# Two hybrid transformer blocks on one core: a spare PSUM bank for a grouped projection's third member, two heads' decays issued after the first linear-attention cores, ScalarE rounding some weights, and one side block moved up

## Chip, cores and metric

One core of one Trainium2 chip runs the whole program. The metric is the device time of one execution in microseconds (us), the median of the runs shown.

## The reference, cut to what matters

The input is one sequence of 512 tokens with 1024 features, float32. Two stacks of two layers follow each other.

- The first stack, per layer: RMS norm with modulation, one wide projection, an RWKV-7 recurrence over 8 heads of 64 (written with chunks of 128 tokens in the kernel), a multi-scale pooling branch, two gated projections, an output projection, and a gated feed-forward network (hidden size 2816).
- The second stack, per layer: RMS norm, one wide projection, gated linear attention (GLA) with 4 heads (key 128, value 256) in both directions, grouped-query attention with 8 query heads, two sigmoid gates, an output projection, a feed-forward network, and a gated side input.

What matters for the change, in the reference's terms (the second stack's GLA branch):

```python
la_f = (jax.nn.log_sigmoid(ra_f @ w_alpha_up[0] + b_alpha[0]) / GLA_TAU).reshape(b, s, GLA_HEADS, GLA_DK)
cum = jnp.cumsum(la, axis=3)
q_dec = q * jnp.exp(cum)
k_intra = k * jnp.exp(-cum)
scores = jnp.where(mask, jnp.einsum('nbhid,nbhjd->nbhij', q_dec, k_intra), 0.0)
o_gla = rms_norm_2(o_f + o_b, g_gla_out)
branch_a = (o_gla * jax.nn.silu(gg)) @ w_o_gla
mixed = jax.nn.sigmoid(gate_a) * branch_a + jax.nn.sigmoid(gate_b) * branch_b
```

The decays of a head (`la`, `cum`) are needed before that head's scores, and the norm of a head's output before its gated output.

## The kernel before, in words

**Weights.** Every large matrix is streamed in 128x128 blocks, four blocks to a chunk, through a ring of 8 slots. SyncE issues a chunk's DMA when the chunk 8 places earlier has been used up (L2265). GpSimd then makes two fp32r tensors of it: `w_hi`, the rounded weight (L2241), and `w_lo`, the rest (L2243), which is written over `raw`. The activations are split in the same way into `_hi` and `_lo`. A block costs three matmuls of 128x512: hi by hi, lo by hi, hi by lo (`linear`, L420 to L422). A projection is 8 blocks, 24 matmuls.

**PSUM.** There are 8 banks. `BANKS` names pools over them: `lin` (banks 0, 1, 2), `bg` (3), `aux` (4 to 7), and in the second stack `lin2` (0, 1) and `bg2` (2, 3). `begin(name, pool)` takes a pool's next bank in turn, and makes TensorE wait until the bank's last reader is done: semaphore `bankN_read` is raised by the instruction that reads the bank last.

**Order.** There is no scheduler: each engine's program is written out by hand, and engines meet at semaphores only. TensorE goes through projections, small matmuls of the recurrences and "side jobs". A side job is a projection whose result is stored to DRAM by ScalarE for later use (`gates_before`, L1114), and whose blocks `fill(n)` deals out, n at a time, at places where TensorE would wait: 8 blocks to a job, L485 to L487.

**Groups.** `group` (through `stepped`, L444, L445, L452) runs the first three projections behind a norm together, block by block, as the norm's output tiles arrive. It is called twice in each layer: for projections `M_WA, M_GL, M_GLV` and the first three of the feed-forward network (`fg0, fu0, fg1`) in the first stack, for `ra, gq, gk` and the first three `pg` of the side input in the second.

**The recurrence of the first stack** (`wkv_chunk`, 4 chunks of 128 tokens in each layer): small matmuls alternate with copies on ScalarE (`gm`, L1236) and products on VectorE (`mt`, L1861, L1863), with one to six fill blocks between them.

**GLA.** TensorE first issues for heads 0 and 1 the projections (`gla_in`: gq, gk, gv, and gg 0 and 1), among them the decay matmuls of all four heads (`gla_decay`, L834, two jobs `gz` each, pool `aux`). ScalarE turns each into logs (L1362 to L1369), VectorE scans them. Then come the cores (`gla_core`), heads 0 to 3, with `gla_in` of head h + 2 behind core h. A core is ten `aux` jobs: two transposes (L846), two scores (L853), three states (L863, L865), `fill(6)`, two outputs `go` 0 and 1 (L877 to L881), `fill(2)`, and the sums of squares `gn` (L888, L889). Then ScalarE takes the root (L1047), VectorE the reciprocal (L1605), and only the product at L2035 releases the bank of `go` 0. In front of each core stand `FILL_CORE[h]` fill blocks. ScalarE makes the factors of head 0 (`gla_factors`, L1380 to L1384) after it has read the last gg projection of `gla_in` 1. Behind core 3 the rest of the first eight side jobs (g2a) is filled, and the output projection `p2a` reads the split head outputs `go_hi`, `go_lo` (L1592).

Of the kernel before, what the change touches and what calls it, by code (L numbers as in the profile page):

```python
# [21 lines left out]
ALU = mybir.AluOpType  # L22
ACT = mybir.ActivationFunctionType
# [36 lines left out]
FILL_SCORE = (0, 2, 0, 5)  # L60
FILL_MEAN = (16, 13)
FILL_POOL = 8
FILL_CORE = (5, 2, 2, 15)
# [57 lines left out]
def emit(nc, known, wstream, ada_slabs, xT, c_rows, cols, consts, rope, inv_count, small, out):  # L121
# [5 lines left out]
    with ExitStack() as ctx:  # L127
# [160 lines left out]
        windows_at = []  # L288

# [68 lines left out]
        def _(pe):  # L358
# [22 lines left out]
            def close(name):  # L381
                closed[name] = len(closed)
                for s in touched:
                    chunk_end[s] = done(name)
                touched.clear()
# [80 lines left out]
            def group(members, key):  # L466

                stepped(members, key, ("lin",) * len(members), "lin")
# [3 lines left out]
            def side_jobs(members, pool):  # L472

                side["jobs"], side["at"], side["pool"] = members, 0, pool
# [212 lines left out]
            def block1(l):  # L687
# [55 lines left out]
                fill(FILL_PREP[l])  # L743
                for c in range(NCH):
                    wkv_chunk(l, c)
# [168 lines left out]
            def block2(l):  # L914
# [4 lines left out]
                side_jobs([(("g2a", l, m), "w_in2", l, N_GA + m) for m in range(DT)], "bg2")  # L919
                gla_in(l, 0, h_in, 0, 1)  # L920
                gla_decay(l, 2)
                gla_in(l, 1, h_in, 3)
                lane[0] = "lin2"
                for h in range(GH):
                    gla_core(l, h)
                    if h + 2 < GH:
                        gla_in(l, h + 2, h_in)
                fill(DT * DT)
# [4 lines left out]
                side_jobs([(("g2b", l, m), "w_in2", l, N_GB + m) for m in range(DT)], "bg2")  # L933
# [85 lines left out]
        def _(act):  # L1019
# [85 lines left out]

            def gates_before(job, stage):

                while stored[0] < len(side_order) and closed[side_order[stored[0]]] < closed[job]:
                    gate = side_order[stored[0]]
                    act.wait_ge(*done(gate))  # L1110
                    if stored[0]:

                        act.wait_ge(sem("gate_out"), 16 * stored[0])
                    ins = af(stage[:], bank_of(gate)[:], ACT.Copy)  # L1114
                    ins.then_inc(bank_read(gate), 1)
                    act.wait_ge(bank_read(gate), turn(gate))
                    act.dma_start(spilled(gate), stage[:]).then_inc(sem("gate_out"), 16)
                    passed("gate_out", gate, by=16)
                    stored[0] += 1
# [252 lines left out]
            def gla_factors(l, h):  # L1372
                for i in range(2):

                    s = (1.0, -1.0)[i] / TAU
                    if h:
                        act.wait_ge(sem("qd_ready"), count("qd_ready", (l, h - 1)))
                    else:
                        act.wait_ge(sem("cum_ready"), count("cum_ready", (l, GH - 1, 1)))
# [56 lines left out]
            def block2(l):  # L1436
# [7 lines left out]
                gla_decay(l, 2)  # L1444
                gla_in(l, 1, 3)
                gla_factors(l, 0)
                for h in range(GH):
                    gla_core(l, h)
                    if h + 2 < GH:
                        gla_in(l, h + 2)  # L1450
                gates_before(("p2a", l, 0), gate_st2)
                act.wait_ge(sem("gate_out"), count("gate_out", ("g2a", l, DT - 1)))
# [115 lines left out]
        def _(dve):  # L1568
# [536 lines left out]
            def block2(l):  # L2105
# [4 lines left out]
                for h in range(GH):  # L2110
                    gla_decay(l, h)
                gla_keys(l, 0)
                for h in range(GH):
                    gla_core(l, h)
                for m in range(DT):
# [89 lines left out]
        def _(pool):  # L2205
# [26 lines left out]

            for s in range(len(chunks)):
# [6 lines left out]
                pool.wait_ge(sem(f"chunk_in{s % RING}"), 16 * (s // RING + 1))  # L2240
                ts(w_hi[:, slot, :], raw[:, slot, :], 1.0, 1.0, ALU.mult, ALU.mult).then_inc(sem("chunk_hi"), 1)  # L2241
                pool.wait_ge(sem("chunk_hi"), s + 1)
# [136 lines left out]
```

## Time and profile before

| | |
|---|---|
| median of 3 runs | 3852.53 us (3851.03 to 3856.24) |
| the profiled execution's own time | 3852.76 us |
| its span, first to last instruction | 3850.8 us |
| PE busy | 3707.2 us, 96% |
| DVE / ACT / POOL busy | 1803.9 / 851.9 / 2275.8 us |
| mean granted TensorE clock | 0.982 |

PE is TensorE, DVE VectorE, ACT ScalarE, POOL GpSimd. The page gives busy time by engine, the chain that ended last, and the costliest groups of instructions. Names in the rows have no buffer numbers. An instruction's row ends, where its engine stood idle before it, with that idle time and what ended it. Matmuls of one stream overlap: a 128x512 matmul shows 0.39 us and the next starts 0.23 us after it; at half clock the starts are 0.43 us apart.

### The profile page before, as it was taken

Reading aid. Unit: us, or ns where it says so; the run is one execution under the profiler, and the core shown is the slowest. Engines: PE = TensorE matmul, PEld = TensorE weight load, DVE = VectorE, ACT = ScalarE, POOL = GpSimd, SP = SyncE. Lnnn points to the kernel's source line nnn. Section 1 sums busy time; section 2 is a strip of 40 time slices with the busy share of each in tenths; the row PEclk is TensorE's granted clock in tenths of the full one; section 3 lists DMA queues with packets and bytes.
Section 4 is the critical chain, followed back from the end, with each engine's and each line's share of the span. In section 5 each row is a group of like instructions: output and inputs, shape, how many; then the busy total and the mean of one; then the engine's idle time right before and its main releaser. Section 6 shows DMA issues by size and latency. Waiting matters only on the chain.

```text
span 3850.8 us, 52946 instructions
## 1 busy us (share of the span) xinstructions
PE 3707.2 (96%) x21300; PEld 3007.9 (78%) x21300; DVE 1803.9 (47%) x2338; ACT 851.9 (22%) x1334; POOL 2275.8 (59%) x2222
## 2 busy tenths in 40 slices
PE   5999999999999999999999999999999999999997
PEld 4887778887787678888887678888778876778886
DVE  5654653234744753124453654523464446453335
ACT  3322110004222110003321532000253225220002
POOL 4613777786513777774656356777645553667773
PEclk9999999999999999998999999999989999999999
DMA  5223444342223443332223132333312331323332
GB/s 187 88 84 108 148 142 145 118 147 77 75 84 108 139 147 109 96 99 64 79 80 118 52 104 83 98 96 98 100 52 83 104 94 55 110 82 98 96 97 70
DMA packets 192483, 386.60 MB, mean 100 GB/s; under 512 B 21488, under 2 KB 21616, under 8 KB 190576
## 3 DMA queue, kind: packets, MB, share of 16 engines
q1 hardware_dynamic: 170064, 338.77, 29.2%
q10 hardware_dynamic: 22176, 44.45, 3.3%
q8 instruction: 170, 2.79, 0.3%
q14 instruction: 73, 0.60, 0.1%
HBM read 362.16 MB, written 20.97 MB: 99 GB/s over the span
## 4 chain that ended last, share of the span: by engine, by line
PE 86%; DVE 9%; ACT 3%; DMA 1%; issue 1%; ACTq 0%; SPq 0%; DVEq 0%
PE psum L420 18%; PE psum L422 18%; PE psum L421 18%; PE psum L485 3%; PE psum L487 3%; PE psum L486 3%; PE psum L507 2%; PE psum L444 2%; PE psum L445 2%; PE psum L452 1%; PE psum L975 1%; PE psum L950 1%; PE psum L604 1%; PE psum L592 1%; PE psum L808 1%; PE psum L809 1%
## 5 line engine op out<-in xcount | busy, mean ns | idle before, releaser
L2241 POOL TENSOR_SCALAR w_hi<-raw 128x512 fp32r<-128x512 f32 x1084 | 745.6, 688 | 1434.4 <-DMA raw<-weight_chunks 1430.8
L2243 POOL TENSOR_TENSOR w_lo<-raw,w_hi 128x512 fp32r<-128x512 f32 x1084 | 1494.3, 1379 | 90.4
L420 PE MATMUL psum<-in_hi,w_hi 128*128 128x512 f32 x1920 | 760.4, 396 | 9.4 <-ACT hs L1319 3.1
L421 PE MATMUL psum<-in_lo,w_hi 128*128 128x512 f32 x1920 | 748.2, 390 | 0.0
L422 PE MATMUL psum<-in_hi,w_lo 128*128 128x512 f32 x1920 | 747.8, 389 | 0.0
L420 PEld LDWEIGHTS psum<-in_hi,w_hi 128*128 128x128 f32 x1920 | 360.8, 188 | 97.6 <-issue 11.1
L421 PEld LDWEIGHTS psum<-in_lo,w_hi 128*128 128x128 f32 x1920 | 360.9, 188 | 79.8 <-issue 6.2
L422 PEld LDWEIGHTS psum<-in_hi,w_lo 128*128 128x128 f32 x1920 | 360.8, 188 | 75.4
L485 PE MATMUL psum<-in_hi,w_hi 128*128 128x512 f32 x576 | 253.9, 441 | 1.5 <-ACT sg L1354 1.5
L486 PE MATMUL psum<-in_lo,w_hi 128*128 128x512 f32 x576 | 225.7, 392 | 0.0
L487 PE MATMUL psum<-in_hi,w_lo 128*128 128x512 f32 x576 | 225.6, 392 | 0.0
L1836 DVE TENSOR_TENSOR hs<-hs,psum 128x512 f32<-128x512 f32 x44 | 30.2, 687 | 299.1 <-PE psum L422 281.9
L2173 DVE TENSOR_TENSOR hs<-psum,rs_t 128x512 f32<-128x512 f32 x88 | 60.8, 691 | 220.4 <-PE psum L422 219.7
L1661 DVE SCALAR_TENSOR_TENSOR ada_col<-ada_col,c_act 128x1024 f32<-128x1024 f32 x80 | 114.9, 1437 | 64.1 <-DMA ada_col<-ada_slabs 61.6
L1319 ACT ACTIVATE hs<-psum 128x512 f32<-128x512 f32 x44 | 26.3, 598 | 531.9 <-PE psum L422 531.8
L485 PEld LDWEIGHTS psum<-in_hi,w_hi 128*128 128x128 f32 x576 | 108.5, 188 | 39.0 <-issue 14.8
L1523 ACT ACTIVATE hs<-hs 128x512 f32<-128x512 f32 x44 | 27.8, 633 | 496.4 <-DVE hs L2173 496.4
L444 PE MATMUL psum<-in_hi,w_hi 128*128 128x512 f32 x288 | 122.4, 425 | 15.1 <-ACT in_hi L1066 6.9
L421 PE MATMUL psum<-hid_lo,w_hi 128*128 128x512 f32 x352 | 136.9, 389 | 0.0
L421 PE MATMUL psum<-h_lo,w_hi 128*128 128x512 f32 x352 | 136.9, 389 | 0.0
L420 PE MATMUL psum<-hid_hi,w_hi 128*128 128x512 f32 x352 | 136.9, 389 | 0.0
L422 PE MATMUL psum<-h_hi,w_lo 128*128 128x512 f32 x352 | 136.9, 389 | 0.0
(421 smaller groups left out, 6759.8 us busy)
## 6 DMA issues: line engine op xcount, KB each, us to landing
raw<-weight_chunks SPq DMA_DIRECT2D x1084, 256.0 KB, 2.6
ada_col<-ada_slabs SPq DMA_DIRECT2D x80, 512.0 KB, 4.1
spill<-gate_st ACTq DMA_DIRECT2D x56, 256.0 KB, 2.7
ada_at<-ada_slabs SPq DMA_DIRECT2D x8, 1024.0 KB, 15.6
gin<-spill ACTq DMA_DIRECT2D x32, 256.0 KB, 3.1
mgs<-spill ACTq DMA_DIRECT2D x32, 256.0 KB, 2.7
sml<-small ACTq DMA_DIRECT2D x4, 1024.0 KB, 5.3
spill<-nt ACTq DMA_DIRECT2D x16, 256.0 KB, 2.6
```

Source lines behind the costliest of these rows:

```text
L420: pe.matmul(bank[:], wh, hi[:, i, :], start=(i == 0), stop=False)
L421: pe.matmul(bank[:], wh, lo[:, i, :], start=False, stop=False)
L422: ins = pe.matmul(bank[:], wl, hi[:, i, :], start=False, stop=(i == len(blocks) - 1))
L444: pe.matmul(banks[n][:], wh, in_hi[:, k, :], start=(k == 0), stop=False)
L445: pe.matmul(banks[n][:], wl, in_hi[:, k, :], start=False, stop=False)
L485: pe.matmul(bank[:], wh, in_hi[:, k, :], start=(k == 0), stop=False)
L486: pe.matmul(bank[:], wh, in_lo[:, k, :], start=False, stop=False)
L487: ins = pe.matmul(bank[:], wl, in_hi[:, k, :], start=False, stop=(k == DT - 1))
L507: ins = pe.matmul(bank[:, t:t + 1], src[:, t * P:(t + 1) * P], kst[:, K_ONES, 0:1], start=(first and t == 0), stop=last, skip_group_check= ...
L1661: ins = stt(buf[:], buf[:], 1.0, c_act[:], ALU.mult, ALU.mult, accum_out=mods[l][:, m:m + 1])
L2241: ts(w_hi[:, slot, :], raw[:, slot, :], 1.0, 1.0, ALU.mult, ALU.mult).then_inc(sem("chunk_hi"), 1)
L2243: ins = tt(w_lo[:, slot, :], raw[:, slot, :], w_hi[:, slot, :].bitcast(F32), ALU.subtract)
```

## The change

1. `group` gives its third member the pool `bg` (bank 3) in place of the third bank of `lin`.
2. In the second stack the decays of heads 2 and 3 are issued on TensorE, ScalarE and VectorE behind cores 0 and 1 in place of among the projections of heads 0 and 1. ScalarE's factors of head h wait for the decays of head max(h, 1), no longer for those of head 3.
3. In the recurrence of the first stack ScalarE makes `w_hi` of the chunks from six behind the start of the recurrence to its end, in place of GpSimd.
4. `FILL_CORE` goes from (5, 2, 2, 15) to (4, 4, 4, 14), and one more side job (`g2b` 0, 8 blocks) is filled in GLA; the fill behind core 3 takes all that is left of nine jobs. The side jobs in attention are seven in place of eight.

```diff
-FILL_CORE = (5, 2, 2, 15)
+CAST_LEAD = 5
+FILL_CORE = (4, 4, 4, 14)
...
+        def scalar_casts():
+            return [s for l in range(len(windows_at)) for s in range(wkv_from[l] + CAST_LEAD + 1, windows_at[l])]
...
             def group(members, key):
-                stepped(members, key, ("lin",) * len(members), "lin")
+                stepped(members, key, ("lin", "lin", "bg"), "lin")
...
-                side_jobs([(("g2a", l, m), "w_in2", l, N_GA + m) for m in range(DT)], "bg2")
+                side_jobs([(("g2a", l, m), "w_in2", l, N_GA + m) for m in range(DT)]
+                          + [(("g2b", l, 0), "w_in2", l, N_GB)], "bg2")
                 gla_in(l, 0, h_in, 0, 1)
-                gla_decay(l, 2)
-                gla_in(l, 1, h_in, 3)
+                gla_in(l, 1, h_in)
                 lane[0] = "lin2"
                 for h in range(GH):
                     gla_core(l, h)
                     if h + 2 < GH:
+                        gla_decay(l, h + 2)
                         gla_in(l, h + 2, h_in)
-                fill(DT * DT)
+                fill(DT * (DT + 1))
...
+            def casts_before(job):
+                while cast_done[0] < len(casts) and casts[cast_done[0]] < closed_at[job] + CAST_LEAD:
+                    s = casts[cast_done[0]]
+                    slot = slice(s % RING * CHUNK, (s % RING + 1) * CHUNK)
+                    act.wait_ge(sem(f"chunk_in{s % RING}"), 16 * (s // RING + 1))
+                    af(w_hi[:, slot, :], raw[:, slot, :], ACT.Copy).then_inc(sem("cast_ready"), 1)
+                    act.wait_ge(sem("cast_ready"), passed("cast_ready", s))
+                    cast_done[0] += 1
             def gates_before(job, stage):
+                casts_before(job)
...
-                    else:
-                        act.wait_ge(sem("cum_ready"), count("cum_ready", (l, GH - 1, 1)))
+                    act.wait_ge(sem("cum_ready"), count("cum_ready", (l, max(h, 1), 1)))
...
-                for h in range(GH):
-                    gla_decay(l, h)
+                gla_decay(l, 0)
+                gla_decay(l, 1)
                 gla_keys(l, 0)
                 for h in range(GH):
                     gla_core(l, h)
+                    if h + 2 < GH:
+                        gla_decay(l, h + 2)
...
+                if s in casts:
+                    pool.wait_ge(sem("cast_ready"), count("cast_ready", s))
+                else:
                     pool.wait_ge(sem(f"chunk_in{s % RING}"), 16 * (s // RING + 1))
-                ts(w_hi[:, slot, :], raw[:, slot, :], 1.0, 1.0, ALU.mult, ALU.mult).then_inc(sem("chunk_hi"), 1)
+                    ins = ts(w_hi[:, slot, :], raw[:, slot, :], 1.0, 1.0, ALU.mult, ALU.mult)
```

Three places in the engines' order. In these rows `psumN` is bank N, and the brackets name the semaphores that the instruction waits for.

TensorE at the end of core 0 of the first GLA layer: L888, L889 (L897, L898 in the change) are `gn`. Before:

```order
L888 MATMUL psum5<-osq_171,kst_56 128x512 [waits osq_ready,bank5_read]
L889 MATMUL psum5<-osq_171,kst_56 128x512
L420 MATMUL psum0<-in_hi_50,w_hi_52 128x512 [waits bank0_read]
```

and in the change, from the first matmul of `go` 0 (L886, `psum7`) and of `go` 1 (`psum4`) on:

```order
L886 MATMUL psum7<-sc_167,gv0_147 128x128 [waits gs_ready,bank7_read,sc_ready]
...
L886 MATMUL psum4<-sc_167,gv0_147 128x128 [waits gs_ready,bank4_read]
...
L897 MATMUL psum5<-osq_171,kst_56 128x512 [waits osq_ready,bank5_read]
L898 MATMUL psum5<-osq_171,kst_56 128x512
L843 MATMUL psum6<-ra_142,sml_57 128x512 [waits bank6_read,bank0_read,small_in]
L843 MATMUL psum7<-ra_142,sml_57 128x512 [waits bank7_read]
L428 MATMUL psum0<-in_hi_50,w_hi_52 128x512 [waits chunk_split,bank0_read]
```

The two decay matmuls of head 2 (L843) now stand between `gn` and the projection of head 2, and the second takes bank 7, which `go` 0 used last.

TensorE at the end of the group `fg0, fu0, fg1` of the first stack's first layer, and the projection `fu1` behind it. Before:

```order
L452 MATMUL psum2<-in_lo_51,w_hi_52 128x512 [waits split_ready]
L452 MATMUL psum0<-in_lo_51,w_hi_52 128x512
L452 MATMUL psum1<-in_lo_51,w_hi_52 128x512
L420 MATMUL psum2<-in_hi_50,w_hi_52 128x512 [waits chunk_split,bank2_read]
```

and in the change:

```order
L460 MATMUL psum1<-in_lo_51,w_hi_52 128x512 [waits split_ready]
L460 MATMUL psum2<-in_lo_51,w_hi_52 128x512
L460 MATMUL psum3<-in_lo_51,w_hi_52 128x512
L428 MATMUL psum0<-in_hi_50,w_hi_52 128x512 [waits chunk_split,bank0_read]
```

`fu1` took the bank that the group's first member had just filled; it now takes one that the group did not use.

ScalarE in the change, in the third chunk of the first layer's recurrence (L1254 and L1260 are the copies `mi` and `gm`, L1138 stores a side job, L1265 copies token rows):

```order
L1254 ACTIVATE mi_87<-psum5 128x512 [waits aux_done,diag_ready]
L1125 ACTIVATE w_hi_52<-raw_53 128x512 [waits chunk_in7,bank5_read]
L1125 ACTIVATE w_hi_52<-raw_53 128x512 [waits chunk_in0,cast_ready]
L1260 ACTIVATE gm_88<-psum6 128x512 [waits aux_done,cast_ready]
L1138 ACTIVATE gate_st_103<-psum2 128x512 [waits gate_out,bg_done,bank6_read]
...
L1260 ACTIVATE gm_88<-psum5 128x512 [waits aux_done]
L1265 ACTIVATE tok0_92<-psum6 128x512 [waits aux_done,bank5_read]
L1125 ACTIVATE w_hi_52<-raw_53 128x512 [waits chunk_in1,bank6_read]
L1260 ACTIVATE gm_88<-psum5 128x512 [waits aux_done,cast_ready]
```

The roundings (L1125) stand in front of the copies `gm`; there are 26 in the program, 13 in each layer, and 26 fewer on GpSimd.

## Rows read from the trace of the kernel before

**Rows 1.** The page, part 4: the chain that ended last, by engine.

```profile
PE 86%; DVE 9%; ACT 3%; DMA 1%; issue 1%; ACTq 0%; SPq 0%; DVEq 0%
```

**Rows 2.** Waits of PE: line waited for, us in total, times, longest.

```profile
PE psum L846 <- DVE kd L1979: 9.2, 2, 4.7
PE psum L579 <- DVE mt L1863: 8.0, 8, 1.5
PE psum L420 <- DVE go_lo L1592: 5.3, 2, 2.8
...
PE psum L420 <- ACT hs L1319: 3.1, 2, 1.6
PE psum L420 <- ACT mg L1553: 3.1, 2, 1.6
PE psum L420 <- ACT wa L1145: 2.1, 2, 1.0
...
PE psum L877 <- DVE gs L2019: 0.6, 1, 0.6
```

**Rows 3.** Timeline, end of the group fg0, fu0, fg1: start, duration (us), instruction.

```profile
551.65 0.84 PE L452 MATMUL psum<-in_lo,w_hi 128*128 128x512 f32 x3
...
554.07 0.50 PE L420 MATMUL psum<-in_hi,w_hi 128*128 128x512 f32 x1 [1.57 <-ACT hs L1319]
```

**Rows 4.** Timeline, behind the group M_WA, M_GL, M_GLV: tanh on ACT, its reader.

```profile
77.03 0.63 ACT L1182 ACTIVATE wa<-wa 64x512 f32<-64x512 f32 x1
...
78.74 0.70 PE L699 MATMUL psum<-wa,sml 64*128 64x512 f32 x2
```

**Rows 5.** Timeline, end of core 0 in the first GLA layer.

```profile
1887.12 1.02 PE L889 MATMUL psum<-osq,kst 128*128 128x512 f32 x2
1887.57 0.80 PE L420 MATMUL psum<-in_hi,w_hi 128*128 128x512 f32 x1
...
1888.22 1.28 ACT L1047 ACT_TABLE_LOAD   x1 [2.48 <-PE psum L889]
...
1889.51 0.69 ACT L1047 ACTIVATE rsg<-psum,eps 128x512 f32<-128x512 f32 x1
1890.30 3.35 DVE L1605 RECIPROCAL rsg<-rsg 128x512 f32<-128x512 f32 x1 [2.18 <-ACT rsg L1047]
...
1893.69 0.75 DVE L2035 SCALAR_TENSOR_TENSOR ot<-psum,col,rsg 128x512 f32<-128x512 f32 x1
```

**Rows 6.** Timeline, one head's decay matmuls (both gz jobs).

```profile
1798.74 1.13 PE L834 MATMUL psum<-ra,sml 16*128 16x512 f32 x4 [0.34 <-issue]
```

**Rows 7.** Timeline, end of core 2, where ScalarE stores a side job before gn.

```profile
1990.72 1.02 PE L889 MATMUL psum<-osq,kst 128*128 128x512 f32 x2
...
1995.95 0.75 DVE L2035 SCALAR_TENSOR_TENSOR ot<-psum,col,rsg 128x512 f32<-128x512 f32 x1
```

**Rows 8.** Timeline, start of core 0: last gg read, factors, first transpose.

```profile
1859.70 0.60 ACT L1354 ACTIVATE sg<-psum 128x512 f32<-128x512 f32 x1 [3.56 <-PE psum L422]
...
1868.69 1.97 PE L846 MATMUL psum<-kst,kd 128*128 128x128 f32 x8 [4.65 <-DVE kd L1979]
```

**Rows 9.** Timeline of PE, then windows (sum; busy by engine; PEclk, DMA, GB/s).

```profile
444.37 0.80 PE L420 MATMUL psum<-yb_hi,w_hi 128*128 128x512 f32 x1 [5.49 <-DVE mt L1811]
...
444.30:450.10 5.80, 5.73 (x14) 4.47 (x15) 3.33 (x7) 1.06 (x1) 0.64 (x1) 0.50 0.24 90
...
1868.60:1872.80 4.20, 4.11 (x19) 4.11 (x20) 0.36 (x2) 2.54 (x5) 1.79 (x2) 0.50 0.02 4
```

**Rows 10.** Timeline, VectorE's first instruction in core 1.

```profile
1924.72 0.69 DVE L1991 TENSOR_TENSOR sc<-psum,kst 128x512 f32<-128x512 f32 x1 [22.47 <-PE psum L853]
```

**Rows 11.** Line L1530: ns min/median/max of an ACT rounding of 128x512.

```profile
L1530 ACT ACTIVATE in_hi<-x x16: 629/632/637, 2739.8 to 3798.4; 128x512 fp32r<-128x512 f32 x16
```

**Rows 12.** Timeline in the recurrence: GpSimd's split and VectorE's mt beside it.

```profile
267.63 1.29 POOL L2243 TENSOR_TENSOR w_lo<-raw,w_hi 128x512 fp32r<-128x512 f32 x1
...
268.15 2.04 DVE L1861 TENSOR_TENSOR mt<-units,kst 64x512 f32<-64x512 f32 x2
```

More of the change, by code:

```diff
@@ L288, in emit @@
         windows_at = []
+        wkv_from = []
+        closed_at = {}
+        def scalar_casts():
+            return [s for l in range(len(windows_at)) for s in range(wkv_from[l] + CAST_LEAD + 1, windows_at[l])]
         def ada_in_ffn(l, mm):
@@ L382, in close @@
                 closed[name] = len(closed)
+                closed_at[name] = len(chunks)
                 for s in touched:
@@ L743, in block1 @@
                 fill(FILL_PREP[l])
+                wkv_from.append(len(chunks))
                 for c in range(NCH):
@@ L932, in block2 @@
                                hi=go_hi, lo=go_lo)
-                side_jobs([(("g2b", l, m), "w_in2", l, N_GB + m) for m in range(DT)], "bg2")
+                side_jobs([(("g2b", l, m), "w_in2", l, N_GB + m) for m in range(1, DT)], "bg2")
                 lane[0] = "lin2"
@@ L1104, in _ @@
             stored = [0]
+            casts = scalar_casts()
+            cast_done = [0]
+            def casts_before(job):
[6 more added lines that the diff above has]
+                    cast_done[0] += 1
             def gates_before(job, stage):
+                casts_before(job)
                 while stored[0] < len(side_order) and closed[side_order[stored[0]]] < closed[job]:
@@ L1443, in block2 @@
                 gla_in(l, 0, 0, 1)
-                gla_decay(l, 2)
-                gla_in(l, 1, 3)
+                gla_in(l, 1)
                 gla_factors(l, 0)
@@ L1449, in block2 @@
                     if h + 2 < GH:
+                        gla_decay(l, h + 2)
                         gla_in(l, h + 2)
                 gates_before(("p2a", l, 0), gate_st2)
-                act.wait_ge(sem("gate_out"), count("gate_out", ("g2a", l, DT - 1)))
+                act.wait_ge(sem("gate_out"), count("gate_out", ("g2b", l, 0)))
                 act.dma_start(rope_t[:], rope).then_inc(sem("rope_in"), 16)
@@ L2114, in block2 @@
                     gla_core(l, h)
+                    if h + 2 < GH:
+                        gla_decay(l, h + 2)
                 for m in range(DT):
@@ L2230, in pool_window @@
                 pool.wait_ge(sem("pooled_ready"), passed("pooled_ready", (l, d)))
+            casts = set(scalar_casts())
             for s in range(len(chunks)):
@@ L2238, in _ @@
                 slot = slice(s % RING * CHUNK, (s % RING + 1) * CHUNK)
-                pool.wait_ge(sem(f"chunk_in{s % RING}"), 16 * (s // RING + 1))
-                ts(w_hi[:, slot, :], raw[:, slot, :], 1.0, 1.0, ALU.mult, ALU.mult).then_inc(sem("chunk_hi"), 1)
-                pool.wait_ge(sem("chunk_hi"), s + 1)
+                if s in casts:
+                    pool.wait_ge(sem("cast_ready"), count("cast_ready", s))
+                else:
+                    pool.wait_ge(sem(f"chunk_in{s % RING}"), 16 * (s // RING + 1))
+                    ins = ts(w_hi[:, slot, :], raw[:, slot, :], 1.0, 1.0, ALU.mult, ALU.mult)
+                    ins.then_inc(sem("chunk_hi"), 1)
+                    pool.wait_ge(sem("chunk_hi"), passed("chunk_hi"))
                 ins = tt(w_lo[:, slot, :], raw[:, slot, :], w_hi[:, slot, :].bitcast(F32), ALU.subtract)
```

## The prediction

> **What bounds the kernel.** I read the chain that ended last first. PE is 86% of it [rows 1], and PE is busy 96% of the span. Work of the other engines therefore counts only where PE stands idle for it, and an idle place that is filled with work taken from a covered place is a gain. So I read next who PE waits for [rows 2]: for `kd` at the start of the first GLA core (9.2 us in two places), for `mt` in the recurrence (8.0 in eight), for the last `go_lo` (5.3 in two), and behind the groups for a copy of the group's first member (3.1, 3.1 and 2.1, two each). Then I followed each place that the change touches in the timeline, and read in the engines' order which bank each moved instruction takes. The number of matmuls is the same before and after; only waits and the clock can move the end.
>
> **The groups.** Before, the projection behind a group takes the bank of the group's first member, which ScalarE has still to read, behind a table load in four of the places. In the feed-forward group the third L452 starts 0.45 us after 551.65, and L420 at 554.07, where 0.23 is the normal step [rows 3]: 1.74 lost, and 0.1 more in the slower first step, so 1.8 us. On bank 0, which the group no longer uses, nothing is waited for, and one projection later (24 steps of 0.23, 5.4 us) the first bank is long read. Four such places (`hs` and `mg`, two each [rows 2]) give 7.2. Behind the first group of the first stack the wait is 1.04, but what follows M_K needs the tanh, which ends at 77.66, while L699 starts at 78.74 [rows 4]: at most 1.0 each, 2.0 for two. The group `ra, gq, gk` has no such wait. **Gain 9.2.** No gain at all would be the other bound, and no row speaks for it.
>
> **The decays behind cores 0 and 1.** This is the large term. The second decay matmul of a head now stands right behind `gn` and takes bank 7. The bank's last reader is VectorE's L2035 on `go` 0, and that comes at the end of a chain: `gn` starts its second half at 1887.12, ScalarE loads a table (1.28) and takes the root (0.69), VectorE the reciprocal (3.35), and L2035 ends at 1893.69 + 0.75 = 1894.44 [rows 5]. Before, PE did not care: it went on with a projection at 1887.57 [rows 5]. Now the first decay job takes some 0.5 us (1.13 for both [rows 6]), and from 1888.1 PE stands until 1894.4: **6.4 us** that it did not wait before. Everything behind on PE's queue waits too, since the queue is in order. Behind core 1 the third side job closes (4 + 8 + 4 + 8 = 24 blocks), so ScalarE stores it before `gn`, as at core 2 of the kernel before, where the table load lies in front: from L889 to the end of L2035 it takes 1996.70 - 1990.72 = 5.98 in place of 7.32 [rows 7], so 5.0 us. Two layers: 2 x (6.4 + 5.0) = **22.8 us**.
>
> What waits behind: ScalarE's decay work (six passes of some 0.65 and two tables of 1.28, 6.5 us [rows 5, 11]) stands in front of its read of the next gq, whose bank is wanted two projections (10.9 us) after the decay matmul: hidden. VectorE's stood idle 22.47 us ahead of core 1 [rows 10], more than its share of one head: hidden. If that cover were gone, core 1 would start late by the excess.
>
> **The clock after these stalls.** After 5.49 us of idling PE ran with a granted clock of 0.50, 1.2 in place of 2.4 GHz, for 5.8 us, and after 4.65 us for 4.2 us [rows 9]. Half of such a stretch is lost: 2.9 and 2.1. I take 2.4 for each of the four, **9.6 us**; the ends are 0 and 4 x 2.9 = 11.6. The Trainium skill (TensorE: Matmul & The Clock Gate, part 1) says that the throttled state is the default and that activity releases it; by that rule all four stalls are paid for twice, and the trace agrees in both places read here.
>
> **The start of core 0.** One would expect the wait for `kd` to go, since ScalarE's factors no longer wait for head 3. But ScalarE reads the last gg projection only at 1859.70, and the factors stand behind that in its program; from there the chain to L846 at 1868.69 runs without a pause [rows 8]. The decays of heads 2 and 3 were not what came last. With 4 fill blocks in place of 5 PE has one block (3 x 0.23 = 0.68) less to do there: **loss 1.4** for two layers. The 0.75 us that the first fill block waited for its bank does go, but into the same wait.
>
> **The other fills.** Two more blocks each ahead of cores 1 and 2, where nothing was waited for: work moved, cost nothing. Core 3 has one fewer, and its `go` waited 0.6 for `gs` in one layer [rows 2]: **loss 1.0** at most. Behind core 3 stand 72 - 58 = 14 blocks in place of 64 - 56 = 8, which is 6 x 0.68 = 4.1 us more cover for a wait of 2.8 and one of 2.5 [rows 2]: both go, with 0.3 us each in steps, and with them a slow-clock stretch of about 1.6 (a smaller case of [rows 9]): **gain 7.3**. In attention the last seven blocks stood behind the last head, as plain work; the first projection there needs the last head's split only in its eighth block, 4.8 us in, so nothing opens.
>
> **ScalarE's roundings.** 26 of some 0.63 us [rows 11]. They stand ahead of copies for which ScalarE waits anyway. If each delayed PE in full, 16.4 us would be lost. On the other side GpSimd's work there falls by a third, and VectorE's two-input work runs long beside it: `mt` took 2.04 beside a GpSimd split [rows 12]. PE's eight waits for `mt` sum to 8.0 [rows 2], that is the bound of the gain. Both are far from likely; nearest are waits of 0.75 at the least, so I take **a gain of 1.0**.
>
> **Sum.** +22.8 + 9.6 + 1.4 + 1.0 - 9.2 - 7.3 - 1.0 = +17.3 us. The profiled execution took 3852.76 us itself, 0.2 over the median of 3852.53, so 3870 us. The bounds of the terms: without the clock 3860, with all bounds of the clock and a third of the roundings' cost 3878.
>
> **Rivals.**
> - *The stalls aren't there* (7%). If bank 7 is free when the second decay matmul comes, or the wait is hidden, the rest of the change stays: -15.1, 3838 us, faster. It decides at 15.1 / 4 = 3.8 us of stall and clock together per place. Against it stands the named semaphore and a chain whose parts have fixed lengths (3.35 of it one instruction) [rows 5].
> - *The clock stays up* (12%): 3860 us. For it: one `go_lo` wait of 2.5 us. Against: both places of [rows 9].
> - *VectorE gets more back* (8%): all of PE's waits for `mt` go, 7 us more, 3863 us. The Trainium skill (SBUF — State Buffer, Who interferes with whom) says that GpSimd and a VectorE instruction with two SBUF inputs lock each other out for a whole instruction. The row of 2.04 agrees, but `w_lo`, the longer of the two GpSimd passes, stays [rows 12].
> - *The first core's wait goes after all* (5%): the 9.2 us for `kd` [rows 2] and the 1.4 are no loss, 3859 us. That is what dropping the wait for head 3 would say; [rows 8] speak against it.
> - *The roundings delay the recurrence* (5%): 16.4 more, 3887 us. ScalarE's copies there are what PE waits for next if they come late; for it only that two roundings in a row stand ahead of one `gm`.
>
> **How the numbers follow.** My forecast has the remaining 63%, around 3870. A measurement of this kernel tells a change from none at about 0.2%, 7.7 us, so slower means over 3860.2 and faster below 3844.8. Slower: the forecast's 63, 8 and 5 of the rivals, half of the 12, and a little of the rest, 82%. Within 0.2%: the other half and the first core's rival, 10%. Faster: the 7 and a little for gains I haven't seen, 8%. The range leaves out the first rival and the last, and reaches from 3857 to 3884.
>
> **What would show it.** Right: four new waits of PE at the second decay matmul (L843) for VectorE's `ot`, some 6.4 and 5.0 us, with PEclk 0.5 behind them; the `hs`, `mg` and `wa` waits behind groups gone; `kd` at the start of core 0 waited for as before or 0.7 us longer (more, with the bank's wait in it); no wait for `go_lo`. Wrong: L843 without idle time, or the waits for `mt` in the recurrence changed by more than 3 us in all, or new waits of PE for ScalarE's `gm`.

## The result and the profile after

The changed kernel takes **3890.24 us** (median of six runs, 3884.73 to 3894.17). The kernel before takes 3855.89 us beside it (3851.03 to 3863.52), so the ratio is **1.0085, interval 1.0069 to 1.0101**: 33 us slower, where +17 to 3870 and a range up to 3884 were forecast. The direction and the place were right, the size was not. In the comparisons below the kernel before has medians of 3854.7 to 3857.7, so the median of three runs on which the forecast was built, 3852.53, was itself some 3 us low. All differences below are ratios to the kernel before on the same chip; 0.001 is 3.9 us.

The page of the changed kernel, parts 1 and 4 (busy us, share, instructions; then the chain that ended last):

```profile
PE 3727.9 (96%) x21300; PEld 3018.2 (78%) x21300; DVE 1788.1 (46%) x2338; ACT 866.1 (22%) x1358; POOL 2255.9 (58%) x2188
...
PE 86%; DVE 10%; ACT 2%; DMA 1%; issue 1%; ACTq 0%; SPq 0%; DVEq 0%
```

PE is the bound as before [rows 1]. Whom it waits for (the view of waits, PE; line waited for, us in total, times, longest):

```profile
PE psum L843 <- DVE ot L2058: 19.8, 4, 5.3
PE psum L855 <- DVE kd L2002: 12.7, 2, 6.4
...
PE psum L587 <- DVE mt L1886: 6.3, 8, 0.8
...
PE psum L886 <- DVE gs L2042: 3.0, 4, 0.9
...
PE psum L428 <- DVE ma L2144: 0.9, 1, 0.9
...
PE psum L428 <- ACT gate_st L1138: 0.7, 1, 0.7
```

Against [rows 2]: the first row is new, four waits at the second decay matmul for VectorE's L2058. The wait for `kd` at core 0 grew from 9.2 to 12.7, by 3.5: 1.5 had stood at the bank of a fill block before (0.75 in each layer), 1.4 is the missing block (0.68 in each layer), and 0.6 is not accounted for. ScalarE's `hs` and `mg` and VectorE's `go_lo` are no longer waited for, nor is ScalarE's `wa` behind the first group, though part of that wait moved to the tanh's reader (L707, 1.2 us in two places). `gs` is waited for four times in place of once, and the waits for `ma` and for a stored gate are new.

One of the four places, PE at the end of core 0 (timeline; start, duration, instruction):

```profile
1880.81 1.02 PE L898 MATMUL psum<-osq,kst 128*128 128x512 f32 x2
1881.76 1.12 PE L843 MATMUL psum<-ra,sml 16*128 16x512 f32 x2
1888.18 2.07 PE L843 MATMUL psum<-ra,sml 16*128 16x512 f32 x2 [5.31 <-DVE ot L2058]
1890.18 0.80 PE L428 MATMUL psum<-in_hi,w_hi 128*128 128x512 f32 x1
1890.78 0.63 PE L429 MATMUL psum<-in_lo,w_hi 128*128 128x512 f32 x1
```

and what it waits for, VectorE in the same stretch:

```profile
1883.99 3.35 DVE L1628 RECIPROCAL rsg<-rsg 128x512 f32<-128x512 f32 x1 [2.18 <-ACT rsg L1057]
1887.38 0.75 DVE L2058 SCALAR_TENSOR_TENSOR ot<-psum,col,rsg 128x512 f32<-128x512 f32 x1
```

L2058 ends at 1888.13, and the second decay matmul starts at 1888.18: the chain of [rows 5], with PE now behind it. In [rows 5] the projection followed the second half of `gn` after 0.45 us; here it follows after 9.37. The matmuls on both sides tell of the clock: the decay pair takes 2.07 us after the wait and 1.12 before it, and L429 takes 0.63 instead of 0.39.

### The profile page after: what moved, and what is told of

The parts are those of the page before. It is cut to its first block, busy times and chain, and to the rows that moved or that the text cites. A ratio compares the mean times of both kernels' runs of the same rounds, so it can differ in the third digit from the quotient of the medians.

```text
span 3884.0 us, 52994 instructions
## 1 busy us (share of the span) xinstructions
PE 3727.9 (96%) x21300; PEld 3018.2 (78%) x21300; DVE 1788.1 (46%) x2338; ACT 866.1 (22%) x1358; POOL 2255.9 (58%) x2188
## 4 chain that ended last, share of the span: by engine, by line
PE 86%; DVE 10%; ACT 2%; DMA 1%; issue 1%; ACTq 0%; SPq 0%; DVEq 0%
PE psum L428 18%; PE psum L430 18%; PE psum L429 18%; PE psum L493 3%; PE psum L495 2%; PE psum L494 2%; PE psum L515 2%; PE psum L452 2%; PE psum L453 2%; PE psum L460 1%; PE psum L985 1%; PE psum L960 1%; PE psum L612 1%; PE psum L600 1%; PE psum L817 1%; PE psum L819 1%
## 5 line engine op out<-in xcount | busy, mean ns | idle before, releaser
L2270 POOL TENSOR_SCALAR w_hi<-raw 128x512 fp32r<-128x512 f32 x1054 | 735.0, 697 | 1251.7 <-DMA raw<-weight_chunks 1247.8
L428 PE MATMUL psum<-in_hi,w_hi 128*128 128x512 f32 x1920 | 763.8, 398 | 1.2 <-DVE ma L2144 0.9
L429 PE MATMUL psum<-in_lo,w_hi 128*128 128x512 f32 x1920 | 752.5, 392 | 0.0
L428 PEld LDWEIGHTS psum<-in_hi,w_hi 128*128 128x128 f32 x1920 | 363.9, 190 | 92.6 <-issue 15.4
L429 PEld LDWEIGHTS psum<-in_lo,w_hi 128*128 128x128 f32 x1920 | 364.1, 190 | 79.8 <-issue 5.3
L493 PE MATMUL psum<-in_hi,w_hi 128*128 128x512 f32 x576 | 252.5, 438 | 0.0
L2198 DVE TENSOR_TENSOR hs<-psum,rs_t 128x512 f32<-128x512 f32 x88 | 60.9, 692 | 223.4 <-PE psum L430 222.7
L429 PE MATMUL psum<-hid_lo,w_hi 128*128 128x512 f32 x352 | 136.9, 389 | 0.0
L430 PE MATMUL psum<-hid_hi,w_lo 128*128 128x512 f32 x352 | 136.9, 389 | 0.0
L428 PE MATMUL psum<-h_hi,w_hi 128*128 128x512 f32 x352 | 136.9, 389 | 0.0
L429 PE MATMUL psum<-h_lo,w_hi 128*128 128x512 f32 x352 | 136.9, 389 | 0.0
```

The costliest lines, as they stand in the source:

```text
L428: pe.matmul(bank[:], wh, hi[:, i, :], start=(i == 0), stop=False)
L429: pe.matmul(bank[:], wh, lo[:, i, :], start=False, stop=False)
L430: ins = pe.matmul(bank[:], wl, hi[:, i, :], start=False, stop=(i == len(blocks) - 1))
L493: pe.matmul(bank[:], wh, in_hi[:, k, :], start=(k == 0), stop=False)
L2270: ins = ts(w_hi[:, slot, :], raw[:, slot, :], 1.0, 1.0, ALU.mult, ALU.mult)
```

## The experiments

Fifteen runs in four groups: eleven different kernels, two of them run twice, and the kernel before twice more. Unless it is said otherwise, an edit is one of the changed kernel; line numbers in the rows are those of the kernel that was run. The times of each run are set against runs of the kernel before made beside it.

**Where do the 33 us come from?** *e1_front* puts the decays of all heads back in front of core 0, on all engines, and ScalarE's wait for the last head's sums with them (TensorE's part is shown):

```
-                gla_in(l, 1, h_in)
+                gla_decay(l, 2)
+                gla_in(l, 1, h_in, 3)
...
-                        gla_decay(l, h + 2)
```

> The changed kernel with the decays of all four heads in front of core 0 again, in all engines' programs (and ScalarE's wait for the last head's sums with them); the group's bank, the roundings, the side block and the fills stay as changed. Theory (the second decay matmul waits for bank 7 at four places, 6.35 and 5.7 us of stretched steps and stall, and the clock behind it): in the profile of the changed kernel the four stretches from gn to the next core grew by 11.7, 11.9, 11.5 and 11.9 us, of which some 2.4 are moved work, so about 37 us go and the kernel takes 3848 to 3856 us, ratio 0.995 to 1.001 to the kernel before; no idle time of PE longer than 1.5 us between gn and the fill blocks of cores 1 and 2. Rival A (the roundings on ScalarE made the loss): the time stays above 3870. Rival B (the fills and the side block made it): the same, above 3870. Both A and B leave idle places in other lines than the decay matmuls.

*e2_late* leaves them between the cores, but behind the gv projections (TensorE's part; ScalarE's program changes in the same way):

```
-                        gla_decay(l, h + 2)
-                        gla_in(l, h + 2, h_in)
+                        gla_in(l, h + 2, h_in, second=h + 2)
```

> The changed kernel with the decays of heads 2 and 3 still behind cores 0 and 1, but behind the gv projections of the next head (some 22 us of PE work later) in place of right behind gn. Theory (it is the bank's last reader, VectorE's first step on go 0, that is waited for, and it is done 6.4 us after gn): no wait at the decay matmuls, 3850 to 3858 us, ratio 0.996 to 1.001, about 35 us under the changed kernel. Rival (whatever the place, decays between the cores cost, since ScalarE's six passes and two tables and VectorE's sums delay the next core): the stall moves to the start of cores 1 and 2 (kd) or to gg's bank, and less than half of the 37 us comes back, 3870 or more.

Measured: e1_front 3852.44 us, ratio **0.9987** (0.9978 to 0.9995); e2_late 3860.50, ratio **1.0002** (0.9994 to 1.0011). Against the changed kernel's 1.0085 that is 38 us (some 7 either way) and 32 us. Roundings and fills are still in both, so the rivals A and B of e1_front fall, and the second run shows that what cost the time is not that the decays stand between the cores, but that they stand right behind `gn`. PE in e1_front at the same place:

```profile
1883.88 1.02 PE L898 MATMUL psum<-osq,kst 128*128 128x512 f32 x2
1884.34 0.80 PE L428 MATMUL psum<-in_hi,w_hi 128*128 128x512 f32 x1
1884.97 0.40 PE L429 MATMUL psum<-in_lo,w_hi 128*128 128x512 f32 x1
```

PE over the two stretches behind cores 0 and 1, first in the changed kernel, then in e1_front (windows; us, busy, PEclk, DMA, GB/s):

```profile
1880.00:1930.00 50.00, 44.69 (x231) 0.93 0.25 71
1944.00:1994.00 50.00, 45.42 (x232) 0.90 0.26 78
```

```profile
1883.00:1923.00 40.00, 40.00 (x229) 1.00 0.32 92
1936.00:1976.00 40.00, 40.00 (x229) 1.00 0.31 97
```

Nearly the same work, with four short decay matmuls more, takes 50 us in place of 40: 5.3 and 4.6 of it idle, the rest in the lower clock and in the matmuls right behind the wait. From the first matmul of `gn` to the next core, the four stretches are 48.10, 48.27, 47.96 and 48.31 us long, and 37.79, 37.79, 37.79 and 37.76 in e1_front; less 1.06 of moved matmuls each, that sums to 37.3 us, against 38 in the timed runs.

What e2_late keeps is 6 us more than e1_front, and its profile has `gs` waits of 7.5 us in six places where e1_front has 2.4 in three: VectorE makes the sums of head 2 until 1927.7 us, past the point where core 1 has its first product for it. *e6_split* therefore has the matmuls behind gq and gk, and ScalarE's part cut in two between its copies of gv (`if t == 0: decay_exp(...)`, `if t == 2: decay_log(...)`).

> The changed kernel with the decay matmuls of heads 2 and 3 behind the gq and gk projections of the next head (10.9 us behind gn, where the chain to the bank's read takes 6.4), and ScalarE's decay work cut in two, behind its copies of gv tiles 0 and 2. In e2_late, with the decays 10 us later still, VectorE did their sums until 1927.7, one us into its work for core 1, and PE waited 7.5 us in six places for gs (2.4 in e1_front). Theory: with the sums 10 us earlier that goes, and the time is e1_front's, ratio 0.998 to 0.9995. Rival: ScalarE's 6.9 us between the copies of gv hold PE at the two banks of gv, 1 to 2 us at each of four places, ratio 1.000 to 1.002.

Measured: 3854.86 us, **1.0000** (0.9991 to 1.0009). The `gs` waits fell to 5.1, but no gain over e2_late can be told from none, so its expected gain (ratio 0.998 to 0.9995) isn't shown.

**What sets the wait for `kd` at core 0?** *e5_late_early* is e2_late with one call moved in ScalarE's program:

```
 def gla_in(l, h, ..., factors=None):
...
+                if factors is not None:
+                    gla_factors(l, factors)
                 for j in range(2):
                     job = ("gg", l, h, j)
...
-                gla_in(l, 1)
-                gla_factors(l, 0)
+                gla_in(l, 1, factors=0)
```

> As e2_late, and in ScalarE's program the factors of head 0 stand ahead of its two last gg copies of head 1, where it stood idle 5.1 us for PE. Theory (my forecast's: the wait for kd at core 0, 6.4 us in each layer, is set by the factors standing behind the last gg copy, not by the decays of heads 2 and 3): kd is ready some 5 to 10 us earlier, the wait goes from 6.4 to under 1 us in both layers, and a part of the half clock behind it; 11 to 15 us less than e2_late, ratio 0.996 to 0.9975. Rival (something else comes last: VectorE's own sums, or the copy of gk): the wait stays over 4 us. Second rival: the copies of gg, now some 6 us later, hold PE at their banks, and half of the gain is given back.

Measured: 3836.82 us, **0.9951** (0.9939 to 0.9964), 20 us under e2_late; run once more as *e15_best_again* (below) it was 3842.78, **0.9967** (0.9955 to 0.9979), 14 under it. ScalarE in e5_late_early:

```profile
1845.98 0.39 ACT L1367 ACTIVATE gv<-psum 128x256 f32<-128x256 f32 x1 [2.21 <-PE psum L819]
1846.38 1.28 ACT L1404 ACT_TABLE_LOAD   x1
...
1850.58 0.20 ACT L1408 ACTIVATE dsc<-dsc 128x3 f32<-128x3 f32 x1
1851.43 1.28 ACT L1379 ACT_TABLE_LOAD   x1 [0.65 <-PE psum L430]
1852.73 0.60 ACT L1379 ACTIVATE sg<-psum 128x512 f32<-128x512 f32 x1
1856.89 0.60 ACT L1379 ACTIVATE sg<-psum 128x512 f32<-128x512 f32 x1 [3.56 <-PE psum L430]
```

The whole factor work (4.4 us, 1846.38 to 1850.78) fits where ScalarE had waited for PE (5.1 us in e2_late), and the gg copies are not held up enough for PE to notice. The view of waits of e5_late_early has no row for `kd` any more; from the first decay matmul to core 0 it takes 60.9 us in both layers, 67.4 in the changed kernel. So the row of 12.7 us above was a matter of ScalarE's order. That the call can stand there at all is owed to the change: by the program, VectorE makes the decay sums in `la`, which the factors write, so with all four heads' decays in front they had to wait for the last head's.

*e7_split_early* joins e6_split and the early factors.

> e6_split and the early factors of e5_late_early together. If both theories hold the gains add: ratio 0.995 to 0.9965, 3838 to 3844 us where the kernel before takes 3857, the fastest so far. If PE's time saved at core 0 is given back at the next wait (sc, gs) or in the clock, 0.997 to 0.999.

Measured: 3841.84 us, **0.9963** (0.9951 to 0.9975), 14 us under e6_split: the moved call is worth about the same there.

**Do the groups gain 9.2 us?** *e3_group* is the kernel before with the third member on bank 3 and nothing else, and *e8_group_again* the same kernel once more:

```
-                stepped(members, key, ("lin",) * len(members), "lin")
+                stepped(members, key, ("lin", "lin", "bg"), "lin")
```

> The kernel before with the third member of a group on bank 3 and nothing else changed. My theory: the waits behind groups for hs and mg go (4 x 1.8 us) and 1.0 each behind the first group of the two stacks, 9.2 us less, ratio 0.9976. Rival (what the trace of the changed kernel hints at: outside of GLA and attention only 5 us were gained in all): part of the gain is given back, because PE reaches the next wait sooner (in the recurrence the next wait ends where it did), 3 to 6 us less, ratio 0.9985 to 0.999.

> The same kernel as e3_group, for a second profile and a narrower interval. In e3_group each of the six places gained what I forecast (1.9 us at hs and mg, 0.8 and 1.0 in the stacks), but between 929 and 944 us PE ran at half clock through the narrow matmuls (64 and 32 rows) where the kernel before ran at full clock, and again from 968, 7.7 us lost in 40. Theory (that drop is chance, not caused by the group): this profile shows a full clock there, or another pattern, and the ratio of the two runs together lies near 0.998, with 9 us less less the chance. Rival (taking away the wait makes the clock drop there, since PE comes there otherwise): the same stretch is slow again and the ratio stays near 0.9994.

Measured: 3856.55 us, 0.9994 (0.9982 to 1.0006), and 3859.08 us, 1.0005 (0.9997 to 1.0014). **Nothing**, although each place gains what was promised. PE at the end of the feed-forward group in e3_group:

```profile
550.54 0.84 PE L452 MATMUL psum<-in_lo,w_hi 128*128 128x512 f32 x3
551.22 0.39 PE L420 MATMUL psum<-in_hi,w_hi 128*128 128x512 f32 x1
```

0.68 us from one to the other in place of 2.42 [rows 3], so 1.74 gained; the other three such places gain the same, and the two behind the first group 1.2 each, 9.3 us in all. It is given back elsewhere. A first part is the tanh's reader L699, which now waits 1.4 us in e3_group and 0.7 in e8_group_again. The rest lies mainly in one stretch. Behind the first group of the first stack's second layer, PE runs four rounds of narrow matmuls (64 and 32 rows); windows of PE in e3_group, in e8_group_again, and in the kernel before:

```profile
925.00:980.00 55.00, 54.66 (x251) 0.84 0.20 53
```

```profile
925.00:980.00 55.00, 54.66 (x250) 0.84 0.19 58
```

```profile
925.00:980.00 55.00, 54.86 (x286) 1.00 0.22 63
```

PE is busy all the time in all three, and has 35 or 36 matmuls fewer done in the same 55 us in the first two. The timeline shows it in the narrow matmuls, e3_group and then the kernel before:

```profile
937.95 2.07 PE L706 MATMUL psum<-gl_s,sml 32*128 32x512 f32 x2
```

```profile
937.15 1.12 PE L706 MATMUL psum<-gl_s,sml 32*128 32x512 f32 x2
```

What it costs can be read between two instructions of VectorE that are the same in both kernels, first in the kernel before, then in e3_group:

```profile
867.27 0.75 DVE L1843 SCALAR_TENSOR_TENSOR x<-psum,mod,x 128x512 f32<-128x512 f32 x1 [5.80 <-PE psum L422]
...
988.25 1.64 DVE L1746 TENSOR_TENSOR b_f<-b_f,qr 128x512 f32<-128x512 f32 x1
```

```profile
864.29 0.75 DVE L1843 SCALAR_TENSOR_TENSOR x<-psum,mod,x 128x512 f32<-128x512 f32 x1 [5.81 <-PE psum L422]
...
993.05 1.70 DVE L1746 TENSOR_TENSOR b_f<-b_f,qr 128x512 f32<-128x512 f32 x1
```

That is 121.0 us and 128.8, although 1.2 us of the group's gain fall inside. e8_group_again has 128.8 too, and the kernel before 122.4 and 120.9 in the two more profiles named below. So about 7.4 us of the 9.3 gained are lost in this one stretch, in both profiles.

To see whether the group's bank brings that on, the kernel before was profiled twice more, and *e11_group_rest* leaves the first group of the stacks on bank 2:

```
+                third = "lin" if key[0] == "n1" else "bg"
+                stepped(members, key, ("lin", "lin", third), "lin")
```

> The kernel before, unchanged, for a second profile. Question: does PE's clock fall among the narrow matmuls of the second stack (929 to 944 us) and behind the token sums of the feed-forward (2737 and 3775 us), where all profiles with the group's bank but two, and all profiles with it, respectively, show at least one such stretch and the one profile of before shows none? Theory A (the group's removed waits bring it on): again none of these. Theory B (chance): one or more of them. 3851 to 3863 us by the runs so far.

> The kernel before a third time, with the same question and the same expectations as e9_before_again: three profiles without a half-clock stretch at 929 to 944, 2737 and 3775 us would make theory A likely, one with such a stretch makes that place chance.

> As e3_group, but the first group of the two stacks (M_WA, M_GL, M_GLV) keeps its third member on bank 2. Of the 9.2 us of local gain 7.2 stay (hs and mg). Theory A (the wait of 1.0 us taken away ahead of the narrow matmuls makes the clock fall there, 7.7 us for a gain of 1.0): no half clock at 929 to 944 us, 3850 us or less, ratio 0.998 or less. Theory B (the clock falls there or elsewhere by chance, or in answer to the other groups): ratio 0.9990 to 1.0005 as in e3_group and e8_group_again.

Measured: before again 3854.41 and 3852.33 us; e11_group_rest 3852.35, 0.9992 (0.9982 to 1.0002). In the window 926 to 946 us the granted clock is 1.00 in all six profiles in which that group has its third member on bank 2, and 0.66 in nine of the eleven in which it is on bank 3 (the other two are e1_front and e4_front_nocast, though up to that point e1_front's program is that of the changed kernel and e4_front_nocast's that of e3_group, and both of those have 0.66). Between the same two instructions of VectorE the nine take 127.8 to 128.9 us and these two 121.9. So there is a link, but it isn't the rule in every run, and how the bank brings it on isn't shown; the wait of 1.0 us that is no longer there ahead of the narrow matmuls is one guess. Theory A's price did not come: e11_group_rest is only 3 us under the mean of the two runs of the whole group, within the error. Its profile says why the difference is small: the stretch takes 124.2 us there, since the clock falls in it at a later place (0.94 granted over 925 to 980 us). And *e12_best*, e5_late_early with the same edit, isn't faster than it: 3841.43 us, 0.9967 (0.9954 to 0.9980).

> As e5_late_early, with the third member of the first group of both stacks back on bank 2. By theory A 4 to 7 us less than e5_late_early, ratio 0.9935; by theory B the same as e5_late_early within 2 us, ratio 0.9945 to 0.996.

The stretches at 2737 and 3775 us, which I had also laid to the group, appear in e9_before_again too (0.91 granted over 2727 to 2747 and 3765 to 3785 us), whose group is on bank 2: those come without the group's bank.

**What are the roundings and the fills worth?** *e4_front_nocast* is e1_front with all roundings on GpSimd; *e13_fills_back* is e5_late_early with the fills and side block of the kernel before; *e14_decays_only* also takes back the group's bank and the roundings. The edit of the fills, here without the line that fills what is left behind core 3:

```
-FILL_CORE = (4, 4, 4, 14)
+FILL_CORE = (5, 2, 2, 15)
...
-                          + [(("g2b", l, 0), "w_in2", l, N_GB)], "bg2")
```

and for the roundings in `scalar_casts`

```
+            return []
```

> As e1_front, and GpSimd does all roundings again: what is left of the change is the group's bank, the side block moved up and the fills. Against e1_front it gives the roundings' worth. My theory: the roundings gain 1 us, so 1 us longer than e1_front. Rival A (they delay the recurrence, each some 0.6 us): e1_front is longer by 5 to 16 us. Rival B (GpSimd and VectorE get out of each other's way): e1_front is shorter by 3 to 8 us, and PE's waits for mt fall with it. Against e3_group it gives the side block and the fills: -7.3 + 1.4 + 1.0 = 5 us less by my forecast; the trace of the changed kernel hints at no gain, since the tail behind the last core took as long with its 4.1 us of added fill as before in one layer, and 4 us longer in the other.

> As e5_late_early with the fills and the side block as in the kernel before (5, 2, 2, 15 blocks ahead of the cores, the first g2b block in attention). Theory A (my forecast's: the moved blocks save 4.9 us, since they cover the wait for go_lo of 2.8 and 2.5 us): 5 us longer than e5_late_early, ratio 0.9965. Theory B (from the stretches of the six profiles: the moved blocks and their covers sum to +2.9 us, as PE waits for gs, ma and the stored gate in their place): 3 us shorter, ratio 0.9935 to 0.995.

> The kernel before with the decays of heads 2 and 3 behind the gv projections of the next head and the factors of head 0 ahead of head 1's gg copies, and nothing else: no member on bank 3, no roundings on ScalarE, fills and side block as before. By the runs so far the group and the rest bring nothing that can be measured; then this is within 3 us of e13_fills_back, ratio 0.994 to 0.9965. If the group's local gain of 9.2 us does come through once the larger waits are gone, e13_fills_back is 6 to 9 us shorter than this.

> e5_late_early again, beside the other two on one chip: 0.994 to 0.9965.

Measured: e4_front_nocast 3853.20 us, 0.9997 (0.9986 to 1.0008); e13_fills_back 3852.32, 0.9990 (0.9981 to 1.0000); e14_decays_only 3857.20, 1.0004 (0.9995 to 1.0013). Against e1_front the first says that the roundings gain 4 us, 5 either way, so neither my 1 nor 0 is excluded; that they cost 5 to 16 us is. PE's waits for `mt` in the recurrence speak for a small gain: 6.3 to 7.2 us in the nine profiles with ScalarE's roundings, 7.7 to 8.5 in the eight without, 1.4 less on the mean. Against e3_group and e8_group_again the same run shows nothing for the fills (1 us less). But against e15_best_again the fills are worth 9 us, some 6 either way: theory A of e13_fills_back had the sign, with 5 us, and theory B had it the wrong way round. What ends PE's waits in e13:

```profile
PE psum L886 <- DVE gs L2040: 5.4, 6, 2.2
...
PE psum L872 <- DVE sc L2012: 4.4, 4, 1.4
PE psum L428 <- DVE go_lo L1613: 4.4, 2, 2.9
```

With VectorE's decay sums between the cores, two fill blocks ahead of cores 1 and 2 are too few. In e13 VectorE ends its sums at 1981.10 and takes the core's first product right behind; PE has by then been waiting for `sc`, until 1981.88. With four blocks that row is 1.2 us, and `go_lo` is gone. The profiles' stretches explain about 3 of the 9 us; the rest isn't located, since e13's profile is 10 us behind e15's before the first place where the two programs differ.

With the old fills, late decays and early factors together bring nothing that can be measured: e14_decays_only has no wait for `kd`, and the time of the kernel before. Its waits for `gs` and `sc` are 5.6 and 5.0 us in their place, and its expected 0.994 to 0.9965 was missed. The group's bank and the roundings together are the difference to e13_fills_back, 5 us, some 5 either way.

## Why the prediction was right, and where it was wrong

**Right:** the sign, the place and the mechanism of the large term. All four waits are there, at the matmul, for the reader and with the chain named; the `hs`, `mg` and `go_lo` waits went. The start of core 0 was read rightly too: the `kd` wait stayed, 6.35 and 6.36 us, since the factors stand behind the last gg read, and e5 shows it. The rival that expected it to go is refuted. The roundings stayed small: PE's waits for `mt` in the recurrence went from 8.0 to 6.3 us, which speaks neither for the rival that wanted all of them gone nor for a delay. The rivals in which the stalls are missing or the clock stays up fell with the first rows above.

**Mis-sized: the four stalls and the clock after them, 32.4 us forecast, 37.3 in the trace and 38 in the runs.** Idle time was 19.8 us, not 22.8. What stands beside it is 17.5 us, where the forecast had 9.6 for the clock. Two things were left out. The first is the decay matmuls themselves: the forecast gave the first job 0.5 us, half of the 1.13 that [rows 6] show for both. Those two jobs ran side by side. Parted by the wait each takes its full time, 1.12 us for the first alone, and the second is 1 us that was not there before. The second is that the half clock begins with this pair, 2.07 us in place of 1.12, another 1 us. With 0.5 us more between `gn` and the first decay matmul that makes some 10 us in the four places. The other 7.5 or so are 7 to 13 slow matmuls of the projection behind, 0.2 us lost on each. So the clock took some 11.5 us where 9.6 were forecast, and 6 us were in no term. The wait at core 1 was also counted from [rows 7], 5.98 us from `gn` to L2035's end; here it is 1951.13 - 1944.48 = 6.65, because ScalarE stores the side job later, 0.61 us before the second half of `gn` in place of 1.30. The Trainium skill (TensorE: Matmul & The Clock Gate, part 1) says that the low rate is the default and that work must first release it. The rows agree: the first work behind each wait ran slow (2.07 against 1.12).

**Wrong: "Gain 9.2. No gain at all would be the other bound, and no row speaks for it."** The six places gain 9.3 us in the trace, and the kernel gains nothing in two comparisons. This is the largest step that failed: a local gain on the bounding engine was carried to the end in full. The clock had rows that spoke for the other bound: by [rows 9] it moves with what PE did before, so taking a pause away at one place can change what is granted at another. In the runs, the stretch with the narrow matmuls takes 7.4 us longer in e3_group and e8_group_again than in the three profiles of the kernel before, with 0.84 of the clock granted over 925 to 980 us in place of 0.97 to 1.00. Another 0.7 to 1.4 us is the wait for the tanh, at its reader in place of behind the group. That the group's bank brings the fall on is borne out by nine of eleven profiles with it against none of six without; why the clock falls there stays open.

**Wrong: the fills, "-7.3", "+1.4" and "+1.0", together 4.9 less.** By e4_front_nocast against the group's runs it is 1 us less (in the order of e5_late_early it is 9, some 6 either way), and by the stretches of the profiles 3 us more (in e1_front and e4_front_nocast it is 152 to 153 us from the first transpose of core 0 to the last `gn`, in place of 148 to 149, where three blocks make 2.05). The waits for `go_lo` went, but new ones came: `gs`, 2.0 to 2.4 us in place of 0.6 at most, `ot` at a core's first products (1.0 to 1.1 us, once), and in the second layer a stored gate (0.7). The wait for `ma` (0.9) isn't of the fills: e3_group has it with the old fills, and only kernels whose first group is on bank 3 have it. "Nothing opens" was read for attention alone.

In sum, of the 16 us between forecast and result: 5 from the stalls and the clock behind them, 9 from the groups and 4 from the fills, less 3 by which the roundings gained more than forecast (4 against 1, by e1_front against e4_front_nocast). That is 15, with an error of some 4 us on most of the terms. e1_front, which is the change without the stalls, is 5 us under the kernel before, where the forecast's other terms made 15.1.

## What to carry to other kernels

Before moving a matmul, ask who read its PSUM bank last and how long that reader's chain is from where the matmul would stand; two projections later (e6_split) or some 22 us later (e2_late) the same matmul had no such wait, and right behind `gn` it cost 9.3 us. The four stalls here, 19.8 us of idle time, cost 37.3 us: nearly twice their length, the instructions right behind them included. A wait of an engine that is late may be its own program order: before covering PE's wait with fill, look for a hole in the late engine's program in which the work fits; one moved call was worth 14 to 20 us here. All three comparisons have four fill blocks ahead of each of the first three cores; with the old fills (e14_decays_only) other waits came in the place of the one that went, and no gain was measured. And gains of 1 to 2 us each, on an engine whose clock can change behind them, are to be measured and not added up.

The version that beats both kernels is e5_late_early: 0.9951 and 0.9967 of the kernel before in two comparisons, some 16 us less than it, and 49 us less than the changed kernel.

## What was unexpected of the hardware

PE's granted clock went to the lower level (1.2 in place of 2.4 GHz) with next to no idle time before it, 0.34 us in e3_group at most: in nine profiles it is 0.66 over the 20 us from 926, with PE busy for 19.65 to 20.00 of them, while narrow matmuls ran (a pair of 32-row ones 2.07 us in place of 1.12). The Trainium skill (TensorE: Matmul & The Clock Gate, part 1) has the gate go by how busy PE has been; by that rule alone the full clock would have stayed, and the trace doesn't agree. What brings it down there stays open: in the other eight profiles the same narrow matmuls ran at 1.00, and no run here varies them. And the same program differs from run to run by more than the small terms of the forecast: e3_group's runs lie between 3841.19 and 3864.25 us, with the same instructions.
